# First-group attention scores as three fp32r products of split Q and K

## The chip, the cores and the metric

The program runs on one core of one Trainium2 chip. The metric is the device time of one execution in microseconds (us); lower is better. Times of the kernel before are the median of 3 runs.

## The reference

Two decoder layers on 256 tokens of width 1024: an mLSTM mixer and a gated ConvFFN, then one shared K/V projection, dilated windowed attention with 16 heads of 64, its output projection, and a second ConvFFN; a final RMSNorm. What the change touches is the attention's score step. There are three groups with (window, dilation) = (128,1), (512,4), (2048,16), each with its own Q, K and V, and for each group and head

```python
q = (rmsnorm(x, norm_g) @ w_q).reshape(Bsz, S, N_GROUPS, B_HEADS, B_HEAD_DIM)
...
s = jnp.einsum('bnqrhe,bnkrhe->bnrhqk', qb, kc).astype(jnp.float32) * (dh ** -0.5) + bias
s = jnp.where(valid, s, -jnp.inf)
m = jnp.max(s, axis=-1, keepdims=True)
p = jnp.exp(s - m)
```

The groups' outputs are merged by their softmax denominators. All tensors are float32.

## The kernel before

**Arithmetic.** Large matmuls run in fp32r, a single-pass form of fp32, as three products of high and low parts: `three` (line 1371) multiplies hi x hi, hi x lo and lo x hi into one PSUM accumulation. The parts are made by ACT, which copies a value into an fp32r tile (the high part), and by DVE or GpSimd, which subtract that high part from the value (the low part). The scores are plain fp32 matmuls of unsplit Q and K.

**Weights.** Weights come in units of 1024 rows by 256 columns through a ring of three slots: SyncE loads `raw`, ACT makes `whi` (`hi`, line 514), DVE or, for one slot in three, GpSimd makes `wlo` (`lo`, lines 872 and 466), PE uses both. One unit gives two tiles, c = 0 and 1, of 24 matmuls each (`tile_of`, line 1578).

**Attention.** Four blocks of four heads, the first three in a loop, the last written out behind it. A block's units on PE follow `BODY` (line 69): j = 0 to 3 are Q and K of groups 1 and 2, j = 4 to 6 the three V, and j = 7 and 8 are Q and K of group 0 (dilation 1) for the next block; the last block has no 7 and 8. The first block's Q and K of group 0 come ahead of the loop. Below, tile (j,c) is part c of unit j. The tiles of a block take three PSUM banks in turn, so a tile can start only when the tile three before it has been read:

```python
pe.wait_ge(ev_done, ev + (c - 2))
ps = bank[qkv_bank(u, c, n < U_BODY)][:, 0:CW]
```

`ev_done` counts the reads. `read_qkv` (line 1325) on DVE reads a tile from PSUM, multiplies it by `rstd` and writes QT, KT or the low part of V.

**Scores.** `scores(t)` (line 1616), t = 0 to 3, serves a pair of heads hp and a half tt of the queries. The two heads lie on partitions 0 to 63 and 64 to 127, so each matmul uses half of PE's rows. Group 0 multiplies 128 queries by all 256 keys; groups 1 and 2, whose tokens are ordered by parity, multiply 128 by the 128 keys of the same parity:

```python
if g == 0:
    ps = ps[:, 0:2, :] if tt else ps[:, 0:4:3, :]
else:
    ps, keys = ps[:, g + tt, :], keys[:, tt, :]
mm = t_.matmul(ps, QT[rows, g, hp, tt * P:(tt + 1) * P], keys,
               start=True, stop=True)
```

Then, for each of a block's 8 slices s: DVE adds the bias (`biased`), ACT takes the exponential (`soft`) and normalises (`normed`), PE transposes (`turned`), ACT and DVE split the result (`p_hi`, `p_lo`). `mixed(0)` and `mixed(1)` multiply by V for heads 0, 1 and 2, 3; `a_cross` (ACT), `a_sum` (DVE), `a_hi` (ACT) and `a_lo` (DVE) turn their result into the split input of the output projection.

**Order.** Every engine's order is written out by hand; instructions of an engine run in that order. PE's at a looped block's end is tile (7,0), tile (7,1), mixed(0), tile (8,0) with turned(7) in its middle, tile (8,1), mixed(1), then the next block's tile (0,0) (lines 1714 to 1719). ACT's is in lines 834 to 849, DVE's in lines 1304 to 1323.

Of the kernel before, what the change touches and what calls it, by code (L numbers as in the profile page):

```python
# [16 lines left out]
P = 128  # L17
# [76 lines left out]
def build(nc, xT, vectors, b_if, a_w_in, a_w_out, w_kv, b_w_q, b_w_out, rel_bias, f_w_up,  # L94
          f_w_down, onehot, mask, group, out):
    ctx = ExitStack()
    with ctx:
# [83 lines left out]
        cb = place("cb", [P, 4, S], F32, ar)  # L181

        ar = [base]
        QT = place("QT", [P, NG, 2, S], F32, ar)
        KT = place("KT", [P, NG, 2, S], F32, ar)
        PT = place("PT", [P, 2, HB, 4, 2, P], F32R, ar)
        Bi = place("Bi", [P, 2, BB, P], F32, ar)
        SB = place("SB", [P, 2, 4 * P], F32, ar)
# [76 lines left out]
        exp_done, linv_done, p_done = sem("exp_done"), sem("linv_done"), sem("p_done")  # L265
        tr_done, pthi_done, ptlo_done = sem("tr_done"), sem("pthi_done"), sem("ptlo_done")
        vhi_done, pv_done = sem("vhi_done"), sem("pv_done")
        cross_done, csum_done, asum_done = sem("cross_done"), sem("csum_done"), sem("asum_done")
        ahi_done, alo_done = sem("ahi_done"), sem("alo_done")

# [72 lines left out]
        def in_bank(t):  # L343

            return 5 if t == 3 else t % 3

        def qkv_bank(u, c, prologue):

# [162 lines left out]
        def _(act):  # L511
# [248 lines left out]
            def block(i, step, last):  # L760

                n0 = U_BODY + (27 if last else 0)
                hb = NHB - 1 if last else i
                def load_bias(h):

                    src = bass.AP(bvd, (hb * HB + h) * (BB * S), [[1, P], [S, BB], [1, P]])
                    act.dma_start(Bi[:, h % 2, :, :], src).then_inc(bi_in[h], 16)

                def soft(s):

                    act.wait_ge(nmx_done, hb * 8 + (s + 1))
                    a.activation(SB[:, s % 2, :], SB[:, s % 2, :], ACT.Exp,
                                 bias=nmx[:, s:s + 1], accum_out=lsum[:, s:s + 1])\
                        .then_inc(exp_done, 1)

                def normed(s):

                    act.wait_ge(linv_done, hb * 8 + (s + 1))
                    a.activation(SB[:, s % 2, :], SB[:, s % 2, :], ACT.Copy,
                                 scale=linv[:, s:s + 1]).then_inc(p_done, 1)  # L780

                def v_hi(j, c):

                    if c:
                        act.wait_ge(w_used[(n0 + j) % RING], rnd(n0 + j, i, step) + 1)
                    else:
                        act.wait_ge(tile_done, hb * 9 + (T_QKV + 2 + j + 1))
                    a.activation(v_part(c, BODY[j][1], 0),
                                 by_head(bank[(2 * (2 + j) + c) % 3][:, 0:S]), ACT.Copy, scale=rstd[:, S + c:S + c + 1]).then_inc(vhi_done, 1)

                def p_hi(s):

                    h, tt = head_of(s)
                    act.wait_ge(tr_done, hb * 8 + (s + 1))
                    a.activation(PT[:, 0, h, :, tt, :],
                                 turned_bank(s).rearrange("p (b q) -> p b q", b=4), ACT.Copy)\
                        .then_inc(pthi_done, 1)

                def a_cross(h):

                    act.wait_ge(pv_done, hb * HB + (h + 1))
                    if h >= 2:
                        act.wait_ge(asum_done, hb * HB + (h - 1))
                    a.activation(cross[own_rows(h), :], pv_out(h, own_rows(h + 1)), ACT.Copy)\
                        .then_inc(cross_done, 1)

                def a_hi(h):

                    act.wait_ge(asum_done, hb * HB + (h + 1))
                    a.activation(*head_out(hb, h, 0), ACT.Copy).then_inc(ahi_done, 1)  # L810


                act.wait_ge(bv_out, 16 * BB)
                load_bias(0)
                load_bias(1)
                for j in range(4):
                    hi(n0 + j + 3, i, step)
                soft(0)
                for m in range(7):
                    if m < 6:  # L820
                        v_hi(4 + m // 2, m % 2)
                    normed(m)
                    if last and m == 6:
                        a_cross(0)
                    soft(m + 1)
                    if m in (1, 2):

                        load_bias(m + 1)
                    p_hi(m)

                    if m and not (last and m > 4):
                        h0 = (m + 1) % 2 * (KD // 2)
                        hi(n0 + 4 + (m - 1) // 2 + 3, i, step, h0, h0 + KD // 2)
                normed(7)
                if not last:
                    hi(n0 + 7 + 3, i, step)
                    a_cross(0)
                a_cross(1)
                p_hi(7)
                a_hi(0)  # L840
                if last:
                    hi(n0 + 9)
                a_hi(1)
                if not last:
                    hi(n0 + 8 + 3, i, step)
                a_cross(2)
                a_cross(3)
                a_hi(2)
                a_hi(3)

            hi(U_QKV + 3)
            root_of(2, S + NT, 7)
            hi(U_QKV + 4)

            act.wait_ge(rstd_done, 3)
            with act.Fori(0, NHB - 1) as i:
# [12 lines left out]
        def _(dve):  # L869
# [356 lines left out]
            def block(i, step, last):  # L1226
# [4 lines left out]
                def evac(j, c):  # L1231
                    if j < 7 or not last:
                        read_qkv(n0 + j, i, step, hb * 9 + (2 + j), 2 + j, c, *BODY[j])

                def biased(s):
# [76 lines left out]
                else:  # L1312
                    a_sum(1)
                    p_lo(7)
                    a_lo(0)
                a_lo(1)
                lo(n0 + 9, i, step)
                evac(8, 0)
                evac(8, 1)
                a_sum(2)  # L1320
                a_sum(3)
                a_lo(2)
# [2 lines left out]
            def read_qkv(n, i, step, m, u, c, kind, g):  # L1325
# [2 lines left out]

                complete(c, m + T_QKV, n, i, step)
                ps = bank[qkv_bank(u, c, n < U_BODY)][:, 0:S]  # L1330
                if kind == "q":
                    o = v.scalar_tensor_tensor(
                        QT[:, g, c, :].rearrange("p (a t) -> p a t", a=NT)[:, :, ::-1],
                        ps.rearrange("p (a t) -> p a t", a=NT), DH ** -0.5,
                        rstd[:, 0:S].rearrange("p (a t) -> p a t", a=NT), ALU.mult, ALU.mult)
                elif kind == "k":
                    o = v.tensor_tensor(KT[:, g, c, :], ps, rstd[:, 0:S], ALU.mult)
                else:
                    dve.wait_ge(vhi_done, (n_v(n) + c + 1) + (i * 6 if step else 0))
                    o = v.scalar_tensor_tensor(v_part(c, g, 1), by_head(ps),  # L1340
# [2 lines left out]
                                               ALU.mult, ALU.subtract)  # L1343
                o.then_inc(ev_done, 1)

            lo(U_QKV + 2)
            rstd_of(2, S + NT)
            for u in range(2):
                if u:
                    lo(U_QKV + u + 2)  # L1350
                for c in range(2):
                    read_qkv(U_QKV + u, 0, 0, u, u, c, "qk"[u], 0)
            with dve.Fori(0, NHB - 1) as i:
                block(i, 9, False)
            block(0, 0, True)
# [12 lines left out]
        def _(pe):  # L1368
# [238 lines left out]
            def block(i, step, last):  # L1607
# [8 lines left out]
                def scores(t):  # L1616
# [4 lines left out]
                        pe.wait_ge(ev_done, hb * 18 + (E_QKV + 12))  # L1621
                    else:
                        pe.wait_ge(smax_done, hb * 8 + (2 * t - 1))
                    for g in range(NG):
                        for j in range(2):
                            rows = slice(j * DH, (j + 1) * DH)
                            ps = score_out(2 * t + j).rearrange("p (b k) -> p b k", b=4)
                            keys = KT[rows, g, hp, :].rearrange("p (b k) -> p b k", b=NT)
                            if g == 0:
                                ps = ps[:, 0:2, :] if tt else ps[:, 0:4:3, :]  # L1630
                            else:
                                ps, keys = ps[:, g + tt, :], keys[:, tt, :]
                            mm = t_.matmul(ps, QT[rows, g, hp, tt * P:(tt + 1) * P], keys,  # L1633
                                           start=True, stop=True)
                            if g == NG - 1:
                                mm.then_inc(sc_done, 1)
# [139 lines left out]
```

## Time and profile before

| | |
|---|---|
| time, median of 3 runs | 764.55 us (764.37 to 764.78) |
| profiled execution | 764.61 us, span 762.9 us |
| PE busy | 750.0 us, 98% of the span |
| DVE busy | 537.9 us, 71% |
| ACT busy | 457.4 us, 60% |
| GpSimd (POOL) busy | 231.8 us, 30% |
| TensorE's granted clock, mean | 0.996 |
| HBM | 178 GB/s over the span |

The span is from the first to the last instruction. PE is the matmul side of TensorE, PEld its weight loads, POOL is GpSimd. In a timeline, a row has an instruction's start and duration in us, and in brackets how long its engine stood idle before it and what released it; neighbours of the same line are merged, with their number behind x. Durations of matmuls overlap, since they are pipelined: the distance of two starts is what counts. Where a row comes from a narrow window, its number behind x counts only what was running in that window. The attention blocks lie between about 310 and 558 us.

### The profile page before, as it was taken

The page shows a single profiled execution, that of the slowest core. Times are in us where ns is not written, and L with a number is a line of the kernel's source. Part 1 is how long each engine was busy: PE and PEld are TensorE (multiplying, and loading weights), DVE is VectorE, ACT ScalarE, POOL GpSimd, SP SyncE. Part 2 cuts the span into 40 slices and gives each one's busy share as a digit, 9 for nine tenths or more (in the row PEclk, how much of TensorE's full clock was granted, in tenths as well). Part 3 has the DMA queues.
Part 4 walks back from the last instruction along what each step waited for, and adds up shares of the span by engine and source line. Part 5 has one row for each costly group of instructions (what it writes and reads, how often), then busy time and mean ns, then how long its engine had stood idle before and what let it go on. Part 6 is the DMA issues. An engine that isn't in the chain of part 4 may idle for free.

```text
span 762.9 us, 16957 instructions
## 1 busy us (share of the span) xinstructions
PE 750.0 (98%) x6446; PEld 737.6 (97%) x6446; DVE 537.9 (71%) x993; ACT 457.4 (60%) x605; POOL 231.8 (30%) x190
## 2 busy tenths in 40 slices
PE   8999999999999999999999999999999999999995
PEld 7999999999999999999999999999999999999994
DVE  5884887888888456547746756766688888887452
ACT  6644567666665566448647647746867566665451
POOL 2351336422223522322322322320214222233321
PEclk9999999999999999999999999999999999999998
DMA  9754265656554665844574284384545656554731
GB/s 286 228 171 128 96 221 176 210 189 197 190 195 153 193 205 172 276 142 143 185 234 144 93 271 145 110 254 142 172 153 180 203 183 215 169 182 140 241 99 55
DMA packets 139805, 136.24 MB, mean 179 GB/s; under 512 B 3585, under 2 KB 139089, under 8 KB 139764
## 3 DMA queue, kind: packets, MB, share of 16 engines
q1 hardware_dynamic: 129016, 130.15, 52.8%
q10 hardware_dynamic: 10748, 5.53, 2.8%
q8 instruction: 27, 0.44, 0.2%
q14 instruction: 14, 0.11, 0.0%
HBM read 134.54 MB, written 1.13 MB: 178 GB/s over the span
## 4 chain that ended last, share of the span: by engine, by line
PE 92%; DVE 3%; ACT 1%; issue 1%; DMA 1%; POOL 0%; SPq 0%; POOLq 0%; DVEq 0%
PE bank L1373 16%; PE bank L1374 15%; PE bank L1375 15%; PE banks L1374 9%; PE banks L1373 9%; PE banks L1375 9%; PE bank L1599 3%; PE bank L1601 3%; PE bank L1600 3%; PE banks L1633 2%; PE banks L1644 2%; PE bank L1405 1%; PE bank L1407 1%; DMA X<-in_xT 1%; PE bank L1406 1%
## 5 line engine op out<-in xcount | busy, mean ns | idle before, releaser
L473 POOL TENSOR_TENSOR wlo<-raw,whi 128x512 fp32r<-128x512 f32 (+1 forms) x165 | 218.2, 1355 | 477.8 <-ACT whi L521 477.8
L521 ACT ACTIVATE whi<-raw 128x2048 fp32r<-128x2048 f32 (+1 forms) x135 | 238.1, 1763 | 178.9 <-PE bank L1375 91.7
L881 DVE TENSOR_TENSOR wlo<-raw,whi 128x1024 fp32r<-128x1024 f32 x163 | 199.3, 1260 | 7.4 <-ACT whi L521 6.5
L1373 PE MATMUL bank<-xsA,whi 128*128 128x256 f32 x568 | 158.6, 279 | 0.9 <-DVE wlo L967 0.9
L1375 PE MATMUL bank<-xsA,wlo 128*128 128x256 f32 x568 | 156.9, 276 | 0.0
L1374 PE MATMUL bank<-xsA,whi 128*128 128x256 f32 x568 | 156.9, 276 | 0.0
L1373 PE MATMUL bank<-xsB,whi 128*128 128x256 f32 x480 | 134.2, 280 | 0.3 <-DVE wlo L881 0.3
L1375 PE MATMUL bank<-xsB,wlo 128*128 128x256 f32 x480 | 132.7, 276 | 0.0
L1374 PE MATMUL bank<-xsB,whi 128*128 128x256 f32 x480 | 132.6, 276 | 0.0
L1373 PEld LDWEIGHTS bank<-xsA,whi 128*128 128x128 f32 x568 | 106.6, 188 | 2.6 <-DVE wlo L967 1.1
L1374 PEld LDWEIGHTS bank<-xsA,whi 128*128 128x128 f32 x568 | 106.7, 188 | 0.1
L1375 PEld LDWEIGHTS bank<-xsA,wlo 128*128 128x128 f32 x568 | 106.6, 188 | 0.0
L1373 PE MATMUL banks<-hs,whi 128*128 128x256 f32 x352 | 97.2, 276 | 0.0
L1374 PE MATMUL banks<-hs,whi 128*128 128x256 f32 x352 | 97.2, 276 | 0.0
L1375 PE MATMUL banks<-hs,wlo 128*128 128x256 f32 x352 | 97.2, 276 | 0.0
L1373 PEld LDWEIGHTS bank<-xsB,whi 128*128 128x128 f32 x480 | 90.1, 188 | 1.5 <-DVE cb L1156 0.5
L1374 PEld LDWEIGHTS bank<-xsB,whi 128*128 128x128 f32 x480 | 90.2, 188 | 0.0
L1375 PEld LDWEIGHTS bank<-xsB,wlo 128*128 128x128 f32 x480 | 90.1, 188 | 0.0
L1374 PEld LDWEIGHTS banks<-hs,whi 128*128 128x128 f32 x352 | 66.1, 188 | 0.0
L1373 PEld LDWEIGHTS banks<-hs,whi 128*128 128x128 f32 x352 | 66.1, 188 | 0.0
L1375 PEld LDWEIGHTS banks<-hs,wlo 128*128 128x128 f32 x352 | 66.1, 188 | 0.0
L1599 PE MATMUL bank<-whi,xsA 128*128 128x256 f32 x192 | 56.7, 296 | 0.0
(201 smaller groups left out, 1521.3 us busy)
## 6 DMA issues: line engine op xcount, KB each, us to landing
raw<-in_f_w_up SPq DMA_DIRECT2D x44, 1024.0 KB, 5.1
raw<-in_w_kv SPq DMA_DIRECT2D x24, 1024.0 KB, 5.7
raw<-in_f_w_down SPq DMA_DIRECT2D x16, 1024.0 KB, 5.2
raw<-in_b_w_q SPq DMA_DIRECT2D x12, 1024.0 KB, 5.2
raw<-in_a_w_in SPq DMA_DIRECT2D x10, 1024.0 KB, 5.9
raw<-in_f_w_down SPq DMA_DIRECT2D x8, 768.0 KB, 4.8
Bi<-bias_by_distance ACTq DMA_DIRECT2D x16, 320.0 KB, 4.7
raw<-in_a_w_out SPq DMA_DIRECT2D x4, 1024.0 KB, 5.4
```

Source lines behind the costliest of these rows:

```text
L473: o = g.tensor_tensor(wlo[s][:, ka:kb, :], raw[s][:, ka * CW:kb * CW] .rearrange("p (k c) -> p k c", c=CW), whi[s][:, ka:kb, :].bitcast(F3 ...
L521: o = a.activation(whi[s][:, k0:k1, :], raw[s][:, k0 * CW:k1 * CW] .rearrange("p (k c) -> p k c", c=CW), ACT.Copy)
L881: v.tensor_tensor(wlo[s][:, ka:kb, :], raw[s][:, ka * CW:kb * CW].rearrange("p (k c) -> p k c", c=CW), whi[s][:, ka:kb, :].bitcast(F32), A ...
L1373: t_.matmul(ps, hi_w, hi_x, start=first, stop=False)
L1374: t_.matmul(ps, hi_w, lo_x, start=False, stop=False)
L1375: return t_.matmul(ps, lo_w, hi_x, start=False, stop=last)
L1405: t_.matmul(ps, xs[:, k, 0, cs], whi[s][:, kk, :], start=first, stop=False)
L1599: t_.matmul(ps, xs[:, k, 0, cs], whi[s][:, k, :], start=first, stop=False)
L1600: t_.matmul(ps, xs[:, k, 0, cs], wlo[s][:, k, :], start=False, stop=False)
L1601: mm = t_.matmul(ps, xs[:, k, 1, cs], whi[s][:, k, :], start=False, stop=last)
L1633: mm = t_.matmul(ps, QT[rows, g, hp, tt * P:(tt + 1) * P], keys, start=True, stop=True)
L1644: mm = t_.transpose(turned_bank(s)[:, to * P:(to + 1) * P], SB[:, s % 2, b * P:(b + 1) * P], ident[:])
```

## The change

Q and K of group 0 get high and low parts (`Q0`, `K0`; QT and KT keep groups 1 and 2), and the group's scores become three fp32r products, hi x hi, hi x lo and lo x hi. Groups 1 and 2 stay as they are. `read_qkv` for Q and K of group 0 now scales the tile in place in PSUM and counts `near_done`; ACT copies the high part (`near_high`, counts `near_hi`); DVE subtracts (`near_low`, counts `ev_done`).

```diff
+        def near_part(kind, c, part):
+            t = QK0["qk".index(kind)][:, part, c, :].rearrange("p (a t) -> p a t", a=NT)
+            return t[:, :, ::-1] if kind == "q" else t
...
@@ ACT, end of a block @@
                 a_cross(1)
                 p_hi(7)
+                near(7, 0)
+                near(7, 1)
                 a_hi(0)
...
                 if not last:
                     hi(n0 + 8 + 3, i, step)
+                near(8, 0)
+                near(8, 1)
                 a_cross(2)
...
+            def near_high(kind, c, b, n):
+                act.wait_ge(near_done, n + near_count(kind, c))
+                a.activation(near_part(kind, c, 0),
+                             bank[b][:, 0:S].rearrange("p (a t) -> p a t", a=NT), ACT.Copy)\
+                    .then_inc(near_hi, 1)
...
@@ ACT, ahead of the loop @@
             root_of(2, S + NT, 7)
+            for c in range(2):
+                near_high("q", c, qkv_bank(0, c, True), 0)
             hi(U_QKV + 4)
+            for c in range(2):
+                near_high("k", c, qkv_bank(1, c, True), 0)
...
@@ DVE, end of a block @@
                     a_sum(1)
                     p_lo(7)
+                    near(7, 0)
+                    near(7, 1)
                     a_lo(0)
...
                 evac(8, 1)
+                if not last:
+                    near(8, 0)
+                    near(8, 1)
                 a_sum(2)
...
+                if kind != "v" and g == 0:
+                    if kind == "q":
+                        o = v.scalar_tensor_tensor(ps, ps, DH ** -0.5, rstd[:, 0:S], ALU.mult,
+                                                   ALU.mult)
+                    else:
+                        o = v.tensor_tensor(ps, ps, rstd[:, 0:S], ALU.mult)
+                    o.then_inc(near_done, 1)
+                    return
...
+            def near_low(kind, c, b, n):
+                dve.wait_ge(near_hi, n + near_count(kind, c))
+                v.tensor_tensor(near_part(kind, c, 1),
+                                bank[b][:, 0:S].rearrange("p (a t) -> p a t", a=NT),
+                                near_part(kind, c, 0).bitcast(F32), ALU.subtract)\
+                    .then_inc(ev_done, 1)
...
@@ PE, scores @@
-                    for g in range(NG):
+                    for n, (pq, pk) in enumerate(((0, 0), (0, 1), (1, 0))):
                         for j in range(2):
                             rows = slice(j * DH, (j + 1) * DH)
                             ps = score_out(2 * t + j).rearrange("p (b k) -> p b k", b=4)
...
+                            t_.matmul(ps[:, 0:2, :] if tt else ps[:, 0:4:3, :],
+                                      QK0[0][rows, pq, hp, tt * P:(tt + 1) * P],
+                                      QK0[1][rows, pk, hp, :].rearrange("p (b k) -> p b k", b=NT),
+                                      start=n == 0, stop=n == 2)
+                    for g in range(1, NG):
...
```

PE's order at the first visit to the scores in the looped block, before; then with the change (QT, KT and Q, K are the stationary and the moving operands; a number in a tile's name is a buffer):

```order
L1601 MATMUL bank<-whi_58,xsA 128x256
L1621 REGISTER_ALU [waits lo_done2]
L1633 MATMUL banks<-KT,QT 128x2x128 [waits ev_done]
L1633 MATMUL banks<-KT,QT 128x2x128
L1633 MATMUL banks<-KT,QT 128x128 x4
L1599 MATMUL bank<-whi_58,xsA 128x256
```

```order
L1660 MATMUL bank<-whi_58,xsA 128x256
L1680 REGISTER_ALU [waits lo_done2]
L1687 MATMUL banks<-K_110,Q_109 128x2x128 [waits ev_done]
L1687 MATMUL banks<-K_110,Q_109 128x2x128 x5
L1695 MATMUL banks<-KT,QT 128x128 x4
L1658 MATMUL bank<-whi_58,xsA 128x256
```

Two matmuls of 256 columns became six; the four of 128 columns stay.

DVE's order at the end of the looped block with the change, from a_sum(0) on (cross is its tile, PT that of p_lo, Q and K those of the new parts, aTs that of a_lo):

```order
L1308 TENSOR_TENSOR cross<-banks,cross 64x256 [waits cross_done]
L1312 TENSOR_TENSOR banks<-banks,cross 64x256 [waits csum_done]
L1299 TENSOR_TENSOR PT<-banks,PT 128x4x128 [waits pthi_done]
L1397 REGISTER_ALU
L1398 TENSOR_TENSOR Q_109<-bank,Q_109 128x2x128 [waits near_hi]
L1397 REGISTER_ALU
L1398 TENSOR_TENSOR Q_109<-bank,Q_109 128x2x128 [waits near_hi]
L1318 ISA [waits ahi_done]
L1318 REGISTER_ALU
L1318 TENSOR_TENSOR aTs<-banks,aTs 64x2x128
```

Before, the two rows into Q and the register rows ahead of them are not there, and the ISA row follows the one into PT; the rest stands in the same order.

ACT's order at the same place with the change:

```order
L820 ACTIVATE cross<-banks 64x256 [waits pv_done] x2
L806 ACTIVATE PT<-banks 128x4x128 [waits tr_done]
L873 REGISTER_ALU
L874 ACTIVATE Q_109<-bank 128x2x128 [waits near_done]
L873 REGISTER_ALU
L874 ACTIVATE Q_109<-bank 128x2x128 [waits near_done]
L826 ISA [waits asum_done]
L826 ACTIVATE aTs<-banks 64x2x128
...
L532 ACTIVATE whi_56<-raw_49 128x2048 [waits w_used0,raw_in0]
L873 REGISTER_ALU
L874 ACTIVATE K_110<-bank 128x256 [waits near_done]
```

Before, L826's rows follow p_hi(7) (the row into PT) at once, and a_cross(2) follows the row into whi.

## Rows read from the trace of the kernel before

**Rows 1.** The page: engine busy times, chain by engine, costliest projection line.

```profile
PE 750.0 (98%) x6446; PEld 737.6 (97%) x6446; DVE 537.9 (71%) x993; ACT 457.4 (60%) x605; POOL 231.8 (30%) x190
...
PE 92%; DVE 3%; ACT 1%; issue 1%; DMA 1%; POOL 0%; SPq 0%; POOLq 0%; DVEq 0%
...
L1373 PE MATMUL bank<-xsA,whi 128*128 128x256 f32 x568 | 158.6, 279 | 0.9 <-DVE wlo L967 0.9
```

**Rows 2.** Source line of the score matmuls: duration min/median/max in ns, forms.

```profile
L1633 PE MATMUL banks<-KT,QT x192: 269/272/480, 333.4 to 543.0; 64*128 64x128 f32 x128, 64*128 64x256 f32 x64
```

**Rows 3.** Timeline of PE, first visit to the scores: start us, us, instruction.

```profile
333.18 0.28 PE L1601 MATMUL bank<-whi,xsA 128*128 128x256 f32 x1
...
333.39 0.70 PE L1633 MATMUL banks<-KT,QT 64*128 64x256 f32 x4
...
333.92 0.50 PE L1633 MATMUL banks<-KT,QT 64*128 64x128 f32 x6
...
334.46 0.38 PE L1599 MATMUL bank<-whi,xsA 128*128 128x256 f32 x1
334.68 0.28 PE L1600 MATMUL bank<-wlo,xsA 128*128 128x256 f32 x1
```

**Rows 4.** Timeline of PE at 42.6 us: 64-row fp32r matmuls of the mLSTM layer.

```profile
42.61 0.38 PE L1488 MATMUL banks<-gmx,selr 64*128 64x256 f32 x1
...
42.84 0.51 PE L1488 MATMUL banks<-gmx,selr 64*128 64x256 f32 x3
43.18 0.63 PE L1491 MATMUL banks<-gmx,selr 64*128 64x256 f32 x4
```

**Rows 5.** Timeline of PE at 122.6 us: two full fp32 passes, then fp32r.

```profile
122.64 0.59 PE L1421 MATMUL banks<-acc,ones 128*128 128x256 f32 x2
...
123.19 0.28 PE L1374 MATMUL bank<-xsA,whi 128*128 128x256 f32 x1
```

**Rows 6.** DVE group of the Q reads; source line of a 256-element ACT write.

```profile
L1332 DVE SCALAR_TENSOR_TENSOR QT<-bank,rstd 128x256 f32<-128x256 f32 x24 | 10.1, 423 | 21.0 <-PE bank L1375 20.4
...
L537 ACT ACTIVATE banks<-X x39: 361/369/389, 11.9 to 751.1; 128x256 f32<-128x256 f32 x27, 128x256 f32 x12
```

**Rows 7.** Timelines of ACT, DVE and PE, end of the first block.

```profile
366.63 0.60 ACT L795 ACTIVATE PT<-banks 128x512 fp32r<-128x512 f32 x1 [0.30 <-PE banks L1644]
367.12 0.38 ACT L810 ACTIVATE aTs<-banks 64x256 f32 x1
...
367.81 0.69 DVE L1264 TENSOR_TENSOR PT<-banks,PT 128x512 fp32r<-128x512 f32 x1
368.41 0.87 DVE L1283 TENSOR_TENSOR aTs<-banks,aTs 64x256 f32 x2
...
367.71 0.28 PE L1375 MATMUL bank<-xsA,wlo 128*128 128x256 f32 x1
367.82 0.28 PE L1373 MATMUL bank<-xsA,whi 128*128 128x256 f32 x1
```

**Rows 8.** Timelines of DVE and PE where PE waits for DVE, 558 us.

```profile
557.65 0.88 DVE L1283 TENSOR_TENSOR aTs<-banks,aTs 64x256 fp32r<-64x256 f32 x2
...
558.58 0.38 PE L1373 MATMUL bank<-aTs,whi 128*128 128x256 f32 x1
558.81 0.28 PE L1374 MATMUL bank<-aTs,whi 128*128 128x256 f32 x1
```

**Rows 9.** Timelines of DVE, ACT and PE behind that block end.

```profile
369.31 3.46 DVE L881 TENSOR_TENSOR wlo<-raw,whi 128x1024 fp32r<-128x1024 f32 x2
...
370.80 1.92 ACT L521 ACTIVATE whi<-raw 128x2048 fp32r<-128x2048 f32 x1 [2.50 <-PE bank L1375]
...
375.11 0.28 PE L1373 MATMUL bank<-xsB,whi 128*128 128x256 f32 x1
```

**Rows 10.** Timelines of ACT and PE ahead of the loop.

```profile
310.38 1.92 ACT L521 ACTIVATE whi<-raw 128x2048 fp32r<-128x2048 f32 x1 [4.13 <-PE banks L1375]
...
312.84 0.28 PE L1373 MATMUL bank<-xsB,whi 128*128 128x256 f32 x1
```

More of the change, by code:

```diff
@@ L183, in build @@
         ar = [base]
-        QT = place("QT", [P, NG, 2, S], F32, ar)
-        KT = place("KT", [P, NG, 2, S], F32, ar)
+        QT = place("QT", [P, NG - 1, 2, S], F32, ar)
+        KT = place("KT", [P, NG - 1, 2, S], F32, ar)
+        QK0 = [place(n, [P, 2, 2, S], F32R, ar) for n in ("Q0", "K0")]
         PT = place("PT", [P, 2, HB, 4, 2, P], F32R, ar)
@@ L267, in build @@
         vhi_done, pv_done = sem("vhi_done"), sem("pv_done")
+        near_done, near_hi = sem("near_done"), sem("near_hi")
         cross_done, csum_done, asum_done = sem("cross_done"), sem("csum_done"), sem("asum_done")
@@ L345, in in_bank, with near_count @@
             return 5 if t == 3 else t % 3
+        def near_part(kind, c, part):
+            t = QK0["qk".index(kind)][:, part, c, :].rearrange("p (a t) -> p a t", a=NT)
+            return t[:, :, ::-1] if kind == "q" else t
+        def near_count(kind, c):
+            return 2 * "qk".index(kind) + c + 1
         def qkv_bank(u, c, prologue):
@@ L797, in p_hi, with near @@
                         .then_inc(pthi_done, 1)
+                def near(j, c):
+                    if not last:
+                        near_high(BODY[j][0], c, (2 * (2 + j) + c) % 3, 4 * hb + 4)
                 def a_cross(h):
@@ L1233, in evac, with near @@
                         read_qkv(n0 + j, i, step, hb * 9 + (2 + j), 2 + j, c, *BODY[j])
+                def near(j, c):
+                    near_low(BODY[j][0], c, (2 * (2 + j) + c) % 3, 4 * hb + 4)
                 def biased(s):
@@ L1319, in block @@
                 evac(8, 1)
+                if not last:
+                    near(8, 0)
+                    near(8, 1)
                 a_sum(2)
@@ L1330, in read_qkv @@
                 ps = bank[qkv_bank(u, c, n < U_BODY)][:, 0:S]
+                if kind != "v" and g == 0:
[6 more added lines that the diff above has]
+                    return
                 if kind == "q":
                     o = v.scalar_tensor_tensor(
-                        QT[:, g, c, :].rearrange("p (a t) -> p a t", a=NT)[:, :, ::-1],
+                        QT[:, g - 1, c, :].rearrange("p (a t) -> p a t", a=NT)[:, :, ::-1],
                         ps.rearrange("p (a t) -> p a t", a=NT), DH ** -0.5,
@@ L1336, in read_qkv @@
                 elif kind == "k":
-                    o = v.tensor_tensor(KT[:, g, c, :], ps, rstd[:, 0:S], ALU.mult)
+                    o = v.tensor_tensor(KT[:, g - 1, c, :], ps, rstd[:, 0:S], ALU.mult)
                 else:
@@ L1348, in _ @@
             for u in range(2):
-                if u:
-                    lo(U_QKV + u + 2)
                 for c in range(2):
                     read_qkv(U_QKV + u, 0, 0, u, u, c, "qk"[u], 0)
+                if u == 0:
+                    lo(U_QKV + 3)
+                for c in range(2):
+                    near_low("qk"[u], c, qkv_bank(u, c, True), 0)
             with dve.Fori(0, NHB - 1) as i:
@@ L1627, in scores @@
                             ps = score_out(2 * t + j).rearrange("p (b k) -> p b k", b=4)
[L1628 to L1633, printed above, removed]
+                            t_.matmul(ps[:, 0:2, :] if tt else ps[:, 0:4:3, :],
[3 more added lines that the diff above has]
+                    for g in range(1, NG):
+                        for j in range(2):
+                            rows = slice(j * DH, (j + 1) * DH)
+                            ps = score_out(2 * t + j).rearrange("p (b k) -> p b k", b=4)
+                            mm = t_.matmul(ps[:, g + tt, :],
+                                           QT[rows, g - 1, hp, tt * P:(tt + 1) * P],
+                                           KT[rows, g - 1, hp, tt * P:(tt + 1) * P],
                                            start=True, stop=True)
```

## The prediction

> **What bounds the kernel now.** I read the page first, then the timeline of TensorE (PE) around one set of scores, and last ACT, DVE and PE at the one place where the changed path meets a wait. PE is busy 98% of the span and 92% of the chain that ended last is PE [rows 1]. Its matmuls stand 0.11 us apart, and the costliest line of its projections has 0.9 us of idle time in front of it in the whole run. So every hundred nanoseconds that the change takes from PE's stream is gained, every wait that it puts into that stream is paid in full, and work on ACT (60% busy) and DVE (71%) costs nothing unless PE waits for it. "Over 0.2%" is 1.5 us here, about what a measurement can tell from no change.
>
> **Part 1, the scores on PE.** One visit to the scores is 6 matmul instructions now; there are 16 visits (4 blocks of heads, 4 each), 96 instructions, and 192 records [rows 2]: an fp32 matmul leaves two, so it runs as two passes. In the visit at 333.39 the 4 passes of the first group take from 333.39 to 333.92, 0.53 us, though each streams 256 columns; the two heads of a pair, in different halves of the array's rows, start together, so that is two pairs of passes at 0.21 each, and 0.11 that is paid once, at entry. The 8 passes of 128 columns after them fill 333.92 to 334.46, four pairs of 0.11 and 0.10 paid at exit, and the first full matmul after them is followed only 0.22 us later instead of 0.12 [rows 3].
> The change replaces the two pairs of the first group by three pairs of single-pass fp32r matmuls of 256 columns. No row shows an fp32r pair on two row halves. The nearest is a run of 64-row fp32r matmuls all on the same half, at 42.6 us: the first takes 0.23, the next three 0.34 together, 0.113 each [rows 4]. So entry costs the same 0.11 in fp32r as in fp32, and a product 0.113. With pairs that start together as the fp32 ones do, the new group takes 0.23 + 2 x 0.113 = 0.45 us against 0.53: a gain of 0.08 a visit. The ends of that cost: 0.43 at best (pairs at the 0.11 of the 128-column passes, gain 0.10); at worst six products one after another, 0.11 + 6 x 0.113 = 0.79 (loss 0.26). I take 0.08, since the 128-column fp32 pairs already show two loads, one on each half, hidden within 0.11 us, and a product of 256 columns in fp32r needs the same 0.11. Going from fp32r to fp32 inside the visit I put at nothing: at 122.64 two fp32 passes and the first full-size fp32r matmul after them take 0.55 us, which is 2 x 0.215 and 0.12 [rows 5]. Sum: 16 x 0.08 = **1.3 us gained**.
> A rule weighed here: the Trainium skill, "TensorE: Matmul & The Clock Gate", Part 3, says that a weight load overlaps a running matmul only when its row group differs. By it, and with that page's estimate of 107 ns for a load of 128 columns, every pair would stand some 0.21 us behind the last, and part 1 would be a loss of about 3.5 us. By that rule, the trace disagrees: the 64-row matmuls of [rows 4] all use one half and still follow each other after 0.113 us.
>
> **Part 2, the wait before tile (8,1).** Today Q and K of the first group leave PSUM in one DVE instruction, which also counts ev_done. Now there are three steps: DVE scales in place, ACT copies the high part, DVE subtracts; ev_done is counted by the last. The instructions are short (a DVE read of a 256-column PSUM tile 0.42 us, a write of one on ACT 0.37 [rows 6], a shorter copy out of PSUM 0.38 [rows 7]); their places matter. In each of the three looped blocks DVE reads tile (7,0), half of the next block's Q, long before anyone asks for its bank. The new low part stands on DVE behind p_lo(7), and PE's tile (8,1), three tiles after (7,0) and so in the same bank, waits until ev_done has counted it.
> From the rows: ACT ends its cross copies, does p_hi(7) at 366.63 and would start the next instruction at 367.12; the two high parts go there, done at 367.50 and 367.9, and are not late. DVE does p_lo(7) at 367.81, and its next instruction starts at 368.41; that is now the low part, done at 368.41 + 0.42 = 368.83. PE starts tile (8,1) at 367.82 today [rows 7]. The delay from a DVE end to PE's start is 0.05 us, and the first matmul after such a wait is followed 0.23 us later, not 0.12, which I take for a weight load that nothing hides: DVE ends at 557.65 + 0.88 = 558.53, PE starts at 558.58 and 558.81 [rows 8]. So the stall is 368.88 - 367.82 = 1.06, and 0.11 with it: 1.17 us a block, **3.5 us** for three. The last block has no unit 7 or 8. The ends: 0.9 if the new DVE step overlaps p_lo(7) more than the next step does today, 1.4 if the register work before each new wait (the order shows one on ACT and on DVE) is not hidden.
> Behind it: what queues on ACT is a_hi(0) and a_hi(1), 0.8 us later; on DVE a_lo(0), a_lo(1) and the weights' low part lo(n0+9), 0.85 later, two new steps. The latter starts at 369.31 and takes 3.46 for its two halves today [rows 9], so it ends by 373.6 at the latest; PE needs the second half 12 matmuls into the next block's first tile, which begins 24 matmuls before 375.11, so at 373.7, and 1.2 later with the stall: 374.9. Hidden, with 1.3 to spare. mixed(1) asks only for p_lo(7) and a_lo(0), and comes 24 matmuls after the start of tile (8,1). The GpSimd and SyncE queues issue what they did before.
> The K parts of unit 8: ACT's hi(n0+11) follows the end of tile (8,1), 370.80 today, 371.97 then, and lasts 1.92; the high part follows by 374.2, the low part by 374.7. PE asks for it at the next block's tile (0,1), 375.11 today and 376.28 then [rows 9]. Hidden, 1.6 us to spare. The a_sum(2) and a_sum(3) behind it come about 1.5 us later than now (0.4 against PE), and nobody waits for them before the next block's mixed.
>
> **Part 3, the first Q and K, ahead of the loop.** Q's low parts come while PE works on K. K's high part on ACT stands behind hi(54), which waits for the last K matmul: 310.38 to 312.30. With the overlap of 0.11 between ACT instructions that [rows 7] shows, the copy ends at 312.58, the low part at 312.63 + 0.42 = 313.05, PE restarts at 313.10. Its tile (0,1), the first to ask, starts at 312.84 today [rows 10]: 0.26 and 0.11 for the exposed load, **0.4 us**.
>
> **The sum.** The profiled execution took 764.61 us (span 762.9), within 0.1 of the median of the runs, 764.55. 764.61 - 1.3 + 3.5 + 0.4 = **767.2 us**, 0.34% slower. With gains of 1.1 to 1.6, stalls of 0.9 to 1.4 a block and 0.2 to 0.6 at the start, the forecast's own range is 765.9 to 768.3.
>
> **Rivals.**
> *A, the new pairs do not run as pairs.* Then a visit loses 0.26 instead of gaining 0.08, 16 x 0.26 = 4.2, and 764.6 + 4.2 + 3.9 = 772.7. For it: no row shows such a pair. Against it: the fp32 pairs do it in every visit. The case in which each pair waits for its own loads lies beside it: a load that is not hidden costs the 0.11 us of [rows 8], so a pair takes 0.22, the group 0.11 + 3 x 0.22 = 0.77, and 16 x 0.24 = 3.8 are lost, 772.3. The row of 64-row matmuls, [rows 4], speaks against it. That is the rule of the Trainium skill weighed above. Together 10%.
> *B, the backlog reaches a second tile.* If ACT and DVE at the block's end are over 1.6 us later than I have it, tile (0,1) of the next block waits too. At half a microsecond and the exposed load that is 0.6 x 3, 769.0. For it: ACT and DVE each get four more instructions there, and ACT waits for DVE and DVE for ACT. Against it: 1.6 us of room. 8%.
> *C, not slower: the entry costs belong to the change of type, not to the row halves.* Place: the first matmul of each visit and the one before it. Today fp32r meets fp32 there; after the change fp32r meets fp32r. If the 0.09 us before the first pass (0.21 instead of 0.12 [rows 3]) and the 0.11 after it were due to the type, and the change of type inside the visit stayed free, each visit would gain 0.08 + 0.20 = 0.28, 4.5 us, and 764.6 - 4.5 + 3.9 = 764.0. It decides from 0.24 a visit on. Against it: [rows 4], where fp32r pays the same at entry, and [rows 5], where a change of type alone is free. The Trainium skill, "TensorEngine Tiling (Array Packing)", Key Properties, says that changing the tiling mode drains the engine, which is the other reading; the trace agrees with 0.21 instead of 0.12. 7%.
> That the change does not do what it says can be left out: the order has ten matmuls a visit where six stood.
>
> **How the numbers follow.** The forecast has 70%, A 10%, B 8%, C 7%, and 5% is for stalls that are much smaller, because something on DVE moves forward that I hold fixed. Slower by over 0.2%, above 766.1: nearly all of the forecast, A and B, together 80%. Within 0.2%: C, half of the rest, and the forecast's low edge, 16%. Faster: 4%. The range leaves out A and C and takes in the forecast's bounds and B: 765.6 to 769.2.
>
> **What would show it.** In the profile after: 96 fp32r records of 64x256 on the first group, pairs 0.11 apart, a visit about 0.08 shorter from the matmul before to the one after. PE idle before tile (8,1) for about 1 us, three times, released by the DVE subtraction into Q, and 0.3 once at about 313 us, released by the one into K; PE's idle time the only larger change, the clock still at full level. The step of part 1 is wrong if the visits grow; that of part 2 if the stall is not there or if PE stops at another tile as well. The whole is wrong if the time is at or below 764.6.

## The result and the profile after

| | before | after |
|---|---|---|
| median, 7 runs each | 764.53 us | 767.26 us |
| lowest to highest | 764.36 to 765.42 | 766.91 to 769.90 |
| ratio | | 1.0039 (95%: 1.0029 to 1.0049) |
| profiled execution | 764.61 us, span 762.9 | 769.90 us, span 768.2 |
| PE, DVE, ACT busy | 750.0, 537.9, 457.4 us | 752.9, 540.9, 462.9 us |

The change costs 2.7 us (by the interval 2.2 to 3.7). The profiled execution of after is the slowest of its seven, 2.6 over their median. What makes it so lies ahead of the change. These are stretches of its span (columns: length, busy time of PE, PEld, DVE, ACT and POOL with their instructions, granted TensorE clock, DMA share, GB/s), and last the first of them again, in the trace of before:

```profile
10.30:17.00 6.70, 6.70 (x24) 4.76 (x23) 6.49 (x12) 5.94 (x12) 0.73 (x1) 0.50 1.13 322
0.00:75.00 75.00, 72.46 (x529) 68.68 (x530) 48.07 (x80) 42.25 (x56) 27.01 (x34) 0.95 0.67 202
75.00:303.00 228.00, 227.75 (x1992) 226.84 (x1991) 173.64 (x298) 140.08 (x175) 80.93 (x62) 1.00 0.57 185
303.00:564.00 261.00, 257.59 (x2259) 250.35 (x2257) 171.59 (x383) 163.67 (x252) 60.53 (x48) 1.00 0.55 171
...
10.30:17.00 6.70, 6.15 (x49) 5.66 (x48) 6.31 (x12) 5.96 (x12) 0.73 (x1) 1.00 1.13 322
```

Between 10.3 and 17.0 us the granted clock of after is 0.50, the lower of its two levels (1.2 GHz), and PE starts 24 matmuls where it starts 49 in before. There they stand 0.21 us apart instead of 0.12 (timeline of PE of after, then of before):

```profile
12.82 0.41 PE L1433 MATMUL bank<-xsA,whi 128*128 128x256 f32 x1
13.04 0.41 PE L1434 MATMUL bank<-xsA,wlo 128*128 128x256 f32 x1
```

```profile
10.70 0.28 PE L1374 MATMUL bank<-xsA,whi 128*128 128x256 f32 x1
10.82 0.28 PE L1375 MATMUL bank<-xsA,wlo 128*128 128x256 f32 x1
```

Why the clock was low there is not shown; the change does nothing before 300 us, and of 32 executions of before in the comparison of place below two (767.18 and 766.74 us) have the same mean clock, 0.991. From 75 us to the end of attention the clock is full in both traces, and behind it the mean is 0.98 in both. The same matmul of the projections that closes the layer before attention comes at 300.50 in the trace of before and at 303.30 in that of after. So the two are compared from there to the first matmul of the output projection that waits for DVE. First before, then after (timeline of PE: start, duration, instruction):

```profile
300.50 0.39 PE L1373 MATMUL bank<-xsB,whi 128*128 128x256 f32 x1
```

```profile
303.30 0.39 PE L1432 MATMUL bank<-xsB,whi 128*128 128x256 f32 x1
...
563.99 0.38 PE L1432 MATMUL bank<-aTs,whi 128*128 128x256 f32 x1
```

The end of that stretch before is the row at 558.58 in [rows 8]. 558.58 - 300.50 = 258.08 us before, 563.99 - 303.30 = 260.69 after: 2.61 us more. The medians differ by 2.73, so this is the effect of the change but for 0.1.

**A visit to the scores**, the first one, as in [rows 3] (timeline of PE; counts as there):

```profile
336.29 0.28 PE L1660 MATMUL bank<-whi,xsA 128*128 128x256 f32 x1
336.50 0.62 PE L1687 MATMUL banks<-K,Q 64*128 64x256 f32 x6
...
336.95 0.49 PE L1695 MATMUL banks<-KT,QT 64*128 64x128 f32 x6
...
337.49 0.39 PE L1658 MATMUL bank<-whi,xsA 128*128 128x256 f32 x1
337.72 0.28 PE L1659 MATMUL bank<-wlo,xsA 128*128 128x256 f32 x1
```

From the last full matmul ahead to the second one behind it is 1.43 us, against 334.68 - 333.18 = 1.50 before. The six products start in pairs: by the start times to the nanosecond at 0 and 4, 223 and 226, 341 and 344 ns from the first. The fp32 part keeps its 0.54 (336.95 to 337.49). By the same start times, the distance plus one matmul more at each end, called the length of a visit from here on, is 1.741 before (1.736 to 1.742 over the 15 visits that a projection tile follows) and 1.664 after (1.662 to 1.668): 0.077 less.

The group of the products in the page has 96 records, half-row in shape, one a product:

```profile
L1687 PE MATMUL banks<-K,Q 64*128 64x256 f32 x96 | 9.9, 312 | 0.0
```

**The end of the first block**, as in [rows 7] (timelines of ACT, DVE, PE):

```profile
369.41 0.60 ACT L806 ACTIVATE PT<-banks 128x512 fp32r<-128x512 f32 x1 [0.29 <-PE banks L1708]
369.90 0.66 ACT L874 ACTIVATE Q<-bank 128x256 fp32r<-128x256 f32 x2
...
370.59 0.69 DVE L1299 TENSOR_TENSOR PT<-banks,PT 128x512 fp32r<-128x512 f32 x1
371.20 0.74 DVE L1398 TENSOR_TENSOR Q<-bank,Q 128x256 fp32r<-128x256 f32 x2
371.86 0.87 DVE L1318 TENSOR_TENSOR aTs<-banks,aTs 64x256 f32 x2
...
370.49 0.28 PE L1434 MATMUL bank<-xsA,wlo 128*128 128x256 f32 x1
371.66 0.39 PE L1432 MATMUL bank<-xsA,whi 128*128 128x256 f32 x1 [0.90 <-DVE Q L1398]
371.89 0.28 PE L1433 MATMUL bank<-xsA,whi 128*128 128x256 f32 x1
```

PE stops for 371.66 - 370.49 = 1.17 us where two matmuls stand 0.11 apart otherwise, and the next follows after 0.23. The ACT copies are long done; DVE starts the low part 0.61 after p_lo(7), and its first half ends at 371.20 + 0.41. The stop is there three times, at 371.66, 434.90 and 498.13. In the waits view of PE it is the one row of that size, and before has none there (300 to 560 us, idle time in total, times, longest):

```profile
PE bank L1432 <- DVE Q L1398: 2.7, 3, 0.9
```

(0.9 is counted from the modelled end of the matmul ahead, 1.17 from its start.)

**Ahead of the loop**, as in [rows 10] (timelines of ACT, DVE, PE):

```profile
313.14 1.92 ACT L532 ACTIVATE whi<-raw 128x2048 fp32r<-128x2048 f32 x1 [1.11 <-PE banks L1434]
...
314.97 0.36 ACT L874 ACTIVATE K<-bank 128x256 fp32r<-128x256 f32 x1
...
315.36 0.42 DVE L1398 TENSOR_TENSOR K<-bank,K 128x256 fp32r<-128x256 f32 x1 [1.85 <-ACT K L874]
...
315.49 0.28 PE L1434 MATMUL bank<-xsB,wlo 128*128 128x256 f32 x1
315.84 0.39 PE L1432 MATMUL bank<-xsB,whi 128*128 128x256 f32 x1
316.06 0.28 PE L1433 MATMUL bank<-xsB,whi 128*128 128x256 f32 x1
```

A gap of 0.35 instead of 0.11 at tile (0,1), right behind the end of K's low part (315.36 + 0.42 = 315.78), and 0.22 instead of 0.11 behind it.

The account, in terms of the prediction's three parts: 3 x (1.06 + 0.11) + (0.24 + 0.11) - 16 x 0.077 = 3.51 + 0.35 - 1.23 = 2.63 us, of 2.61.

### The profile page after: what moved, and what is told of

Same layout as the page of the kernel before. It is cut to its first block, busy times and chain, and to the rows that moved or that the text cites. A ratio compares the mean times of both kernels' runs of the same rounds, so it can differ in the third digit from the quotient of the medians.

```text
span 768.2 us, 17077 instructions
## 1 busy us (share of the span) xinstructions
PE 752.9 (98%) x6478; PEld 739.8 (96%) x6478; DVE 540.9 (70%) x1009; ACT 462.9 (60%) x621; POOL 228.9 (30%) x190
## 4 chain that ended last, share of the span: by engine, by line
PE 90%; DVE 4%; ACT 3%; issue 2%; DMA 1%; ACTq 0%; POOL 0%; POOLq 0%; DVEq 0%
PE bank L1432 15%; PE bank L1433 15%; PE bank L1434 15%; PE banks L1433 9%; PE banks L1432 9%; PE banks L1434 9%; PE bank L1658 3%; PE bank L1660 3%; PE bank L1659 3%; PE banks L1708 2%; ACT whi L532 1%; PE banks L1687 1%; PE bank L1464 1%; PE bank L1466 1%; PE bank L1465 1%
## 5 line engine op out<-in xcount | busy, mean ns | idle before, releaser
L484 POOL TENSOR_TENSOR wlo<-raw,whi 128x512 fp32r<-128x512 f32 (+1 forms) x165 | 215.3, 1338 | 485.6 <-ACT whi L532 485.6
L912 DVE TENSOR_TENSOR wlo<-raw,whi 128x1024 fp32r<-128x1024 f32 x163 | 196.8, 1244 | 6.7 <-ACT whi L532 6.1
```

Source lines behind the costliest of these rows:

```text
L484: o = g.tensor_tensor(wlo[s][:, ka:kb, :], raw[s][:, ka * CW:kb * CW] .rearrange("p (k c) -> p k c", c=CW), whi[s][:, ka:kb, :].bitcast(F3 ...
L912: v.tensor_tensor(wlo[s][:, ka:kb, :], raw[s][:, ka * CW:kb * CW].rearrange("p (k c) -> p k c", c=CW), whi[s][:, ka:kb, :].bitcast(F32), A ...
```

## The experiments

The account leaves open whether the waits are a matter of place or the price of the three-step reads, whether the 0.077 is what the products are worth, and why pairs and entry cost what they do. All times are medians; "before" is the kernel before in the same comparison.

### The parts apart

**products**, the PE side without the chain of reads:

```diff
-                        o = v.scalar_tensor_tensor(ps, ps, DH ** -0.5, rstd[:, 0:S], ALU.mult,
-                                                   ALU.mult)
+                        o = v.scalar_tensor_tensor(near_part(kind, c, 0), wide[0], DH ** -0.5,
+                                                   wide[1], ALU.mult, ALU.mult)
                     else:
-                        o = v.tensor_tensor(ps, ps, rstd[:, 0:S], ALU.mult)
-                    o.then_inc(near_done, 1)
+                        o = v.tensor_tensor(near_part(kind, c, 0), *wide, ALU.mult)
+                    o.then_inc(ev_done, 1)
...
-                    for n, (pq, pk) in enumerate(((0, 0), (0, 1), (1, 0))):
+                    for n, (pq, pk) in enumerate(((0, 0), (0, 0), (0, 0))):
```

(`wide` is ps and rstd in two halves; near_high and near_low do nothing.)

> The products alone: DVE reads Q and K of the first group in one step into the high part and counts ev_done at once, with no ACT copy and no subtraction; all three products take the high parts (the low parts of the first group's Q and K are left out, so its scores lose precision and count thrice). Same matmuls on PE as the changed kernel. Theory (the products gain 0.077 us a visit and the reads cost only the waits): 764.5 - 1.2 = 763.3 us, no wait before tile (8,1). Rival (the visits' gain is lost on PE elsewhere): 764.5.

763.33 us (12 runs, 763.20 to 764.09) against 764.74 before, ratio 0.9980 (95%: 0.9972 to 0.9989). No gap at tile (8,1) or (0,1) is in its trace, and the visits are the 1.66 of after. The products alone gain what their visits show.

**chain**, the reads without the products:

```diff
-                    for n, (pq, pk) in enumerate(((0, 0), (0, 1), (1, 0))):
+                    for n in range(1):
...
-                                      QK0[0][rows, pq, hp, tt * P:(tt + 1) * P],
-                                      QK0[1][rows, pk, hp, :].rearrange("p (b k) -> p b k", b=NT),
-                                      start=n == 0, stop=n == 2)
+                                      QK0[0][rows, 0, hp, tt * P:(tt + 1) * P].bitcast(F32),
+                                      QK0[1][rows, 0, hp, :].bitcast(F32)
+                                      .rearrange("p (b k) -> p b k", b=NT), start=True, stop=True)
```

> The three-step reads alone: as the changed kernel, but the first group's scores are one fp32 matmul of the high parts per head, as many and as long as before (the low parts of Q and K are left out of the scores). Theory: the visit is as long as in the kernel before, 1.74 us, the two waits stay, and the time is 764.5 + 3.9 = 768.4 us, 1.2 over the changed kernel. Rival (the products gain nothing): 767.2.

768.60 us (4 runs, 768.23 to 769.44), ratio 1.0049 (1.0033 to 1.0066): 4.1 over the 764.51 of before, where 3.9 was expected. The first group's records are those of an fp32 matmul again, 64 and up to 480 ns (source line of the score matmuls in the trace of chain; duration min/median/max):

```profile
L1687 PE MATMUL banks<-K,Q x64: 376/428/480, 334.5 to 547.2; 64*128 64x256 f32 x64
```

Its visits last 1.74 as in before, and the gaps of 1.17 (at 369.92, 433.56 and 497.19) and 0.35 (at 313.82) are there. The waits view of PE has the row of after again:

```profile
PE bank L1432 <- DVE Q L1398: 2.7, 3, 0.9
```

So the two parts add up: -1.4 by products and +4.1 by chain give 2.7, what after costs. (The intervals are wide beside that: 0.8 to 2.1 gained, 2.5 to 5.0 lost.)

### Place or price

**place** moves unit 7's parts forward on both engines:

```diff
                 normed(7)
                 if not last:
+                    near(7, 0)
+                    near(7, 1)
                     hi(n0 + 7 + 3, i, step)
...
                 p_hi(7)
-                near(7, 0)
-                near(7, 1)
...
                 evac(7, 1)
+                if not last:
+                    near(7, 0)
+                    near(7, 1)
                 a_sum(0)
...
                     p_lo(7)
-                    near(7, 0)
-                    near(7, 1)
```

> The changed kernel with the high and low parts of unit 7's tiles moved forward: on ACT behind the last normalisation and ahead of the weights' high part, on DVE behind the second read of unit 7 and ahead of a_sum(0), where DVE stood idle for 2.6 us. Theory (the stall before tile (8,1) is the place of the low part behind p_lo(7), 1.17 us three times): PE no longer waits there, 767.3 - 3.5 = 763.8 us, about 0.7 under the kernel before. Rival (the stall is the price of the three-step read itself, or the ACT copies push a_cross and p_lo(7) back by 0.75 and PE waits at mixed(1) or the next block instead): 766 to 767.

763.69 us (11 runs, 763.49 to 764.10), ratio 0.9983 (0.9975 to 0.9992) to before: 3.6 less than after, and the sign is turned: 1.05 under its own before. Timelines of DVE, ACT and PE of place at the end of the first block:

```profile
364.26 0.76 DVE L1399 TENSOR_TENSOR Q<-bank,Q 128x256 fp32r<-128x256 f32 x2 [0.62 <-ACT Q L874]
366.76 0.42 DVE L1308 TENSOR_TENSOR cross<-banks,cross 64x256 f32<-64x256 f32 x1 [1.74 <-ACT cross L820]
...
368.60 0.69 DVE L1299 TENSOR_TENSOR PT<-banks,PT 128x512 fp32r<-128x512 f32 x1
...
367.15 0.60 ACT L806 ACTIVATE PT<-banks 128x512 fp32r<-128x512 f32 x1
...
367.95 0.28 PE L1435 MATMUL bank<-xsA,wlo 128*128 128x256 f32 x1
368.06 0.28 PE L1433 MATMUL bank<-xsA,whi 128*128 128x256 f32 x1
368.17 0.28 PE L1434 MATMUL bank<-xsA,whi 128*128 128x256 f32 x1
```

DVE makes the low parts in time in which it stood idle, and still idles 1.74 us after them. p_hi(7) no longer waits for PE: ACT reaches it late, as the rival said, and p_lo(7) is late too: it starts at 368.60, 0.54 behind the start of tile (8,1) at 368.06, and no longer holds that tile up. mixed(1) is far off. PE runs through with 0.11 between matmuls. The stall was the place.

**late** goes the other way, with the low parts one step further back:

```diff
-                    near(7, 0)
-                    near(7, 1)
                     a_lo(0)
+                    near(7, 0)
+                    near(7, 1)
```

> The changed kernel with the low parts of unit 7 one instruction later on DVE, behind a_lo(0). It adds to the suspected wait. Theory (PE pays every hundred nanoseconds of it): the gap before tile (8,1) grows from 1.18 by one DVE step of 0.44 in each of three blocks, 767.3 + 1.3 = 768.6 us. Rival (the wait has another cause, so that DVE's order does not set it): 767.3.

768.49 us (4 runs, 767.97 to 768.91), 1.2 more than after where 1.3 was expected. Timelines of DVE and PE of late:

```profile
368.18 0.41 DVE L1318 TENSOR_TENSOR aTs<-banks,aTs 64x256 f32 x1
368.51 0.74 DVE L1398 TENSOR_TENSOR Q<-bank,Q 128x256 fp32r<-128x256 f32 x2
...
367.47 0.28 PE L1434 MATMUL bank<-xsA,wlo 128*128 128x256 f32 x1
368.97 0.39 PE L1432 MATMUL bank<-xsA,whi 128*128 128x256 f32 x1 [1.23 <-DVE Q L1398]
```

The gap is 1.50, 0.33 more, three times: 1.0 us. The step was sized at 0.44; in this place DVE's steps follow each other after 368.51 - 368.18 = 0.33. The low part starts 0.33 later behind p_lo(7) than in after, and the gap grows by as much: PE pays DVE's delay one for one.

**pro** moves one ACT instruction ahead of the loop:

```diff
+            near_high("k", 0, qkv_bank(1, 0, True), 0)
             hi(U_QKV + 4)
-            for c in range(2):
-                near_high("k", c, qkv_bank(1, c, True), 0)
+            near_high("k", 1, qkv_bank(1, 1, True), 0)
```

> The changed kernel with only the first K's high part, part 0, put ahead of the third weights' high part on ACT before the loop. Theory: the 0.35 us of wait and exposed load at the first block's tile (0,1) goes, 766.9 us, and nothing else moves; in the profile the gap of 0.35 between two matmuls at about 313 us is 0.11. Rival (DVE, with two more steps for Q ahead, is what is late): the gap stays, 767.3.

766.97 us (7 runs, 766.87 to 767.26), 0.3 below after. The times alone do not show that (ratio to before 1.0028, 1.0017 to 1.0038, against 1.0029 to 1.0049 for after); the trace does: the gap of 0.35 is gone, the three of 1.18 are not.

**both** is place and pro together.

> Both moves together: the changed kernel with unit 7's parts early and the first K's part early. Theory: what is left of the change is the gain on PE, 16 visits at 0.077 us, so 764.5 - 1.2 = 763.3 us, faster than before by 0.16%. If the extra ACT and DVE work costs anything beyond the two waits, it is over 763.6.

763.45 us (12 runs, 763.18 to 765.55), ratio 0.9983 (0.9974 to 0.9991). By the medians it is 1.3 under the 764.74 of before, 3.8 under after, and within 0.15 of products, which has neither ACT copies nor subtractions. With both moves the additional work on ACT and DVE costs nothing that can be measured. This is the version to use.

### What a pair is, and what an entry is

**serial** swaps the two loops around the products:

```diff
-                    for n, (pq, pk) in enumerate(((0, 0), (0, 1), (1, 0))):
-                        for j in range(2):
+                    for j in range(2):
+                        for n, (pq, pk) in enumerate(((0, 0), (0, 1), (1, 0))):
```

> The changed kernel with the two loops around the three products swapped, so that one head's three come on one half of the rows before the other head's three. It prices pairs that do not run as pairs. Theory (only neighbours on different halves start together): five or six product times of 0.113 instead of three, 0.23 to 0.34 us more a visit, 3.6 to 5.4 in all, 770.9 to 772.7 us. Rival (each half has its own queue and the order does not matter): 767.2. By the rule that a load waits for the matmul of its own half, each product would stand 0.22 behind the last and the visit would be 0.9 longer, over 780.

767.22 us (6 runs, 767.02 to 767.38), after's time. The expectation failed. Timeline of PE of serial, first visit:

```profile
333.87 0.39 PE L1687 MATMUL banks<-K,Q 64*128 64x256 f32 x2
...
334.21 0.28 PE L1687 MATMUL banks<-K,Q 64*128 64x256 f32 x2
334.32 0.28 PE L1695 MATMUL banks<-KT,QT 64*128 64x128 f32 x2
```

Three products of one head are followed by three of the other in the program, and still the records start two at a time, at 0 and 10, 223 and 233, 341 and 351 ns from the first. A visit lasts 1.67. The simplest reading is that each half takes its own matmuls in order and does not wait for the other's; the records do not say which head each belongs to.

**one_half_all** puts all score matmuls of both heads on one half:

```diff
-                            rows = slice(j * DH, (j + 1) * DH)
+                            rows = slice(0, DH)
...
-                            rows = slice(j * DH, (j + 1) * DH)
+                            rows = slice(0, DH)
```

> The changed kernel with every score matmul of both heads, fp32r and fp32, on the same half of the rows, 0 to 63 (the second head's scores are left out, the first head's stand in their place). It prices what running in pairs is worth, which the run with swapped loops did not. Theory (pairs run together because they sit on different halves): three more product times of 0.113 and four more passes of 0.11 a visit, 0.78 us, 767.3 + 12.5 = 779.8 us, with steps of 0.11 between single records instead of between pairs. By the rule that a weight load waits for the running matmul of its own half, the products and passes stand 0.22 apart, 2.3 more a visit, over 800. Rival (what bounds a visit is not the array's halves): 767.3.

779.30 us (4 runs, 779.04 to 779.42), ratio 1.0187 (1.0170 to 1.0204). Timeline of PE, first visit:

```profile
333.66 0.28 PE L1660 MATMUL bank<-whi,xsA 128*128 128x256 f32 x1
333.87 0.38 PE L1687 MATMUL banks<-K,Q 64*128 64x256 f32 x1
...
334.09 0.75 PE L1687 MATMUL banks<-K,Q 64*128 64x256 f32 x5
334.68 1.05 PE L1695 MATMUL banks<-KT,QT 64*128 64x128 f32 x8
```

The five products from 334.09 take 0.59, 0.118 each, one at a time; the first record to the second is 0.22, as in [rows 4]. A visit lasts 2.46 where after's lasts 1.66, 0.80 more, and 16 x 0.80 = 12.8 is 0.8 more than the 12.0 between the medians. Three gaps that after has ahead of transposes that wait for the softmax, 0.36 at 403.4 and at 466.6 and 0.47 at 548.3, are 0.14, 0.14 and 0.20 in this trace; that is 0.22 + 0.22 + 0.27 = 0.7 of it. Running in halves is therefore worth 12 us here, and a load on a half is hidden behind that half's own running matmul, in fp32r and in fp32. (Both heads now load the same columns of Q; but in [rows 4] each of the four matmuls loads other columns, and they stand 0.113 apart too.) A version with only the products on one half and the fp32 matmuls on both has no result: matmuls of the two halves would have written the same PSUM bank with nothing to order them. The price of the products alone is therefore read here: 334.68 - 333.87 = 0.81 us for six.

**fp32_first** puts the fp32 groups ahead of the products (the increment of sc_done moves to the last product):

```diff
+                    for g in range(1, NG):
+                        for j in range(2):
...
+                            t_.matmul(ps[:, g + tt, :],
...
                     for n, (pq, pk) in enumerate(((0, 0), (0, 1), (1, 0))):
...
+                            if n == 2:
+                                mm.then_inc(sc_done, 1)
```

> The changed kernel with the two fp32 groups ahead of the three products in each visit: the same matmuls, but now fp32r meets fp32 at entry and fp32r meets fp32r at exit. Theory (the 0.1 us steps at entry and exit belong to the change between full and half rows): same time, 767.2 within 0.3, and steps of about 0.21 before and 0.11 extra behind, as before. Rival (they belong to the type): the steps move from one end to the other, and if they are not equal the time moves by over 0.5.

767.40 us (6 runs, 767.18 to 767.62), the same. Timeline of PE of fp32_first, start and end of the first visit (the row at 333.57 is the first fp32 pair):

```profile
333.36 0.28 PE L1660 MATMUL bank<-whi,xsA 128*128 128x256 f32 x1
333.57 0.38 PE L1687 MATMUL banks<-KT,QT 64*128 64x128 f32 x2
...
334.57 0.39 PE L1658 MATMUL bank<-whi,xsA 128*128 128x256 f32 x1
334.80 0.28 PE L1659 MATMUL bank<-wlo,xsA 128*128 128x256 f32 x1
```

333.36 to 334.80 is 1.44, as 1.43 in after. The entry into fp32 costs 0.21, as the entry into the products does in after (336.29 to 336.50), and the exit from the products costs the same 0.23 behind its first full matmul as the exit from fp32. The steps belong to the change between full and half rows; rival C is out.

## Why the prediction was right

Each of its three terms came as forecast, so the sum is not right by errors that cancel.

- **Part 1, 1.3 us gained**: 1.23 by the visits (0.077 for 0.08), and products alone is 1.4 below before by the medians, with an interval of 0.8 to 2.1. Products 0.11 apart, pairs together, entry unchanged: each of these was a reading of rows from another place and held. The reason given for the pairs was incomplete: it spoke of neighbours on different halves, and serial shows that they need not be neighbours in the program. That an fp32 matmul runs as two passes is a reading of its two records; at 256 columns each of them takes 0.21, nearly twice an fp32r product of that width, and no run takes it further apart.
- **The rule weighed there**: the Trainium skill, "TensorE: Matmul & The Clock Gate", Part 3, says that a load overlaps a running matmul only when its row group differs. By that rule, the trace disagrees: one_half_all tests it directly, and the products on one half stand 0.118 apart, not at the 0.22 that the expectation worked out from it.
- **Part 2, 1.17 us a block**: measured 1.06 more in front of the tile and 0.11 behind its first matmul, three times. The reasoning was a chain of starts on DVE; the start of the low part after p_lo(7) was forecast at 0.60 and is 0.61. place and late show that this chain sets the stall, from both sides.
- **Part 3, 0.4 us**: 0.35. From the end of the weights' high part on ACT to PE's restart it is 0.78 (315.06 to 315.84), forecast 0.80 (312.30 to 313.10); the copy took 0.36 and started 0.09 before the end of its predecessor, where 0.11 was assumed.
- **Hidden work**: the parts of unit 8, and everything queued behind the new steps, delayed nothing, so rival B did not happen. products and both have the same time, which is the direct test.
- **Rivals A and C** were tested by one_half_all and fp32_first. A's condition is not met: the products run in pairs. Its price was right: six products one after another take 0.81 from the first, where it had 0.79.
- **The sum**: 767.2 forecast, 767.26 measured. The profiled execution alone would have been misleading, with 2.8 us of a slow start ahead of the change (303.30 against 300.50).

## What to carry to other kernels

When the bound engine runs without gaps, split an edit into what it does to that engine's stream and where its new steps stand in the other engines' queues; the second was three times the first here, and moving three pieces of it turned 0.39% slower into 0.17% faster. A buffer that was read early and is now released by the last of three steps should have those steps placed where the engine that does them idles, before anything that depends on later work of the bound engine. To price a form that the trace lacks, look for the same shape elsewhere in the kernel: four half-row matmuls at 42 us, with the pairing taken from the fp32 rows, gave the gain of a visit to within a few nanoseconds.

## What the runs showed that was not expected

- Program order between the two halves of the rows does not matter: three products of one head and then three of the other run as three pairs, 0.11 apart, in 1.67 us a visit, against 1.66 with the heads in turn.
- On one half, products of 256 columns in fp32r follow each other after 0.118 us and passes of 128 columns in fp32 after 0.11, loads included, so the two halves save the second head's time (0.80 a visit, where 0.78 was worked out) and nothing else.
- A start can cost 2.8 us more in one execution than in another: at a granted clock of 0.50 from 10.3 to 17.0 us PE does half the matmuls that it does at 1.00. Some of that comes back: by the end of the stretch the trace of after is 4.0 us behind that of before, and 2.7 at 21 us, because PE of before then stands idle for 0.89 us at 17.34, waiting for DVE, and PE of after does not.
